# RWKV inverse in a backbone step: the transposed half made by transposes on the whole array, and three groups staggered

## The reference, cut to what matters

```python
def step(S, inp):
    r_t, w_t, k_t, v_t, kk_t, a_t = inp
    S = (S * w_t[:, :, None, :]
         - jnp.einsum('bhvk,bhk->bhv', S, kk_t)[..., None] * (kk_t * a_t)[:, :, None, :]
         + v_t[..., None] * k_t[:, :, None, :])
    return S, jnp.einsum('bhvk,bhk->bhv', S, r_t)
```

## Time and profile before

| | |
|---|---|
| time, median of 3 runs | 2682.11 us (2679.97 to 2689.62) |
| the profiled execution: its time | 2688.59 us |
| its span | 2686.8 us, 60164 instructions |
| PE busy | 2465.4 us (92%), 26965 matmuls |
| DVE / ACT / POOL busy | 1139.0 / 550.7 / 243.6 us |
| mean granted clock of PE, share of full speed | 0.977 |
| one lap of the RWKV loop (first L1367 to the next lap's) | 1382.68 to 1457.06, 74.38 us |

### The profile page before, as it was taken

The page is one execution under the profiler, slowest core; times in us unless marked ns, Lnnn a source line. Parts: engine busy times, 40 slices in busy tenths (PEclk is TensorE's granted clock), DMA queues, the critical chain, the costliest instruction groups (busy, mean ns, idle before and its releaser), DMA issues.

```text
span 2686.8 us, 60164 instructions
## 1 busy us (share of the span) xinstructions
PE 2465.4 (92%) x26965; PEld 1887.9 (70%) x26965; DVE 1139.0 (42%) x2084; ACT 550.7 (20%) x1099; POOL 243.6 (9%) x166
## 2 busy tenths in 40 slices
PE   6999889999999989987888888879899999999995
PEld 3666566777776757746667776766789778987794
DVE  4534687554563366646555555626300000000004
ACT  3101222000010020025545445431200000000002
POOL 0000240000000000003333222120100000000001
PEclk9999999999999999999999999998999999999997
DMA  8640133321221112310000000003366565656554
GB/s 353 264 185 32 48 137 133 131 79 63 72 88 60 64 57 102 127 71 4 23 23 23 23 23 24 6 20 143 125 221 214 206 220 209 239 195 221 203 202 151
DMA packets 59027, 321.20 MB, mean 120 GB/s; under 512 B 8368, under 2 KB 17968, under 8 KB 28208
## 3 DMA queue, kind: packets, MB, share of 16 engines
q1 hardware_dynamic: 46304, 281.32, 28.7%
q10 hardware_dynamic: 9040, 19.67, 1.9%
q0 software_dynamic: 3456, 16.78, 1.6%
HBM read 288.38 MB, written 29.36 MB: 118 GB/s over the span
## 4 chain that ended last, share of the span: by engine, by line
PE 85%; DVE 6%; issue 4%; ACT 3%; DMA 2%; SPq 0%; POOL 0%; DVEq 0%; ACTq 0%; POOLq 0%
PE PS L1008 36%; PE PS L1672 17%; PE PS L1696 6%; PE PS L1697 3%; PE PS L1270 2%; PE PS L1410 2%; PE PS L1416 1%; PE PS L1340 1%; PE PS L1390 1%; PE PS L971 1%; PE PS L1480 1%; PE PS L674 1%; DMA arena<-in_k 1%; PE PS L1401 1%; PE PS L1105 1%
## 5 line engine op out<-in xcount | busy, mean ns | idle before, releaser
L1008 PE MATMUL PS<-arena,ring 128*128 128x320 f32 x2680 | 742.4, 435 | 18.7 <-DVE arena L2635 13.4
L1008 PEld LDWEIGHTS PS<-arena,ring 128*128 128x128 f32 x2680 | 509.2, 191 | 239.5 <-issue 17.8
L1672 PE MATMUL PS<-arena,ring 128*128 128x192 f32 x2816 | 461.1, 327 | 4.0 <-issue 4.0
L1672 PEld LDWEIGHTS PS<-arena,ring 128*128 128x128 f32 x2816 | 458.8, 190 | 7.0 <-issue 7.0
L2911 DVE TENSOR_TENSOR arena<-arena,PS 128x192 f32<-128x192 f32 x88 | 31.1, 354 | 435.7 <-ACT arena L2119 435.7
L1696 PE MATMUL PS<-ring,arena 128*128 128x512 f32 (+1 forms) x384 | 155.1, 559 | 0.5 <-DMA ring<-in_exd 0.5
L1008 PE MATMUL PS<-arena 128*128 128x320 f32 x536 | 151.1, 432 | 0.0
L1008 PEld LDWEIGHTS PS<-arena 128*128 128x128 f32 x536 | 101.9, 190 | 42.4
L1696 PEld LDWEIGHTS PS<-ring,arena 128*128 128x128 f32 x384 | 71.6, 190 | 74.8 <-issue 71.9
L909 POOL TENSOR_TENSOR arena<-arena,const 128x512 f32<-128x512 f32 (+1 forms) x24 | 23.1, 962 | 1090.4 <-DVE arena L2738 752.1
L2119 ACT ACTIVATE arena<-PS 128x192 f32<-128x192 f32 x88 | 29.0, 330 | 420.9 <-PE PS L1672 420.9
(11 more groups left out here) (356 smaller groups left out, 3208.5 us busy)
## 6 DMA issues: line engine op xcount, KB each, us to landing
ring<-in_k SPq DMA_DIRECT2D x145, 1024.0 KB, 4.8
arena<-in_k SPq DMA_DIRECT2D x47, 1024.0 KB, 11.4
ring<-in_exd SPq DMA_DIRECT2D x32, 1408.0 KB, 5.9
ring<-in_ffd SPq DMA_DIRECT2D x8, 1408.0 KB, 5.9
rkv_s<-arena ACTq DMA_DIRECT2D x24, 320.0 KB, 4.3
expert_rows<-arena POOLq DMA_DIRECT2D x4, 1536.0 KB, 10.3
x<-in_x SPq DMA_DIRECT2D x2, 2560.0 KB, 9.7
expert_rows<-arena ACTq DMA_DIRECT2D x8, 512.0 KB, 2.6
```

The source lines that it names most:

```text
L1008: m = pe.matmul(out, lhs[:, k], rhs[:, k], start=k == 0, stop=k == count - 1)
L1672: m = pe.matmul(PS[:, k % 4, t * CAP:(t + 1) * CAP], w[:, kt, t * P:(t + 1) * P], xe[:, kt], start=kt == 0, stop=kt == KT - 1)
```

## The change

The transposed half of the inverse is no longer carried along by products of its own. X is kept for a pair of units side by side (a 128x128 block: two units by two heads), and in each level ten transposes of whole 128x128 blocks (four, four and two for the groups) turn it (`turn_inverse`, L1370 of the changed file). ACT copies the turned block out, and the products that make the next X (L1381; L1383 at level 64) use it. The products L1416 and the start by `xt`, M and `sides` go, and with them the two halves in every second level. The steps of a level are no longer in blocks by kind; the table `TURNS` gives their order over the groups, on PE and on ACT. Heads and units are placed on the array's quarters by another rule (`heads[r]`, bank `+ h`) in Y, X, `Q` and `MV`.

```diff
+TURNS = (("Y", 0), ("Y", 1), ("T", 0), ("Y", 2), ("T", 1), ("X", 0), ("T", 2), ("X", 1), ("X", 2))
...
-        XX = r(UNITS, 2, HD)
+        XX = r(UNITS // 2, 2, 2, HD)
...
+        inverse = lambda v: XX[:, v // 2, 0, v % 2]
+        turned_inverse = lambda v, h: XX[heads[v % 2], v // 2, 1, (v ^ h) % 2]
+        beside = lambda v, h: v - v % 2 + h
...
-                    masks.wait(pool, f"off2{i}", j)
-                    masks.done(pool.tensor_tensor(of_pair(XX[:, :, 1], i), eyes(i), of_pair(LTm[:, 0], i), ALU.subtract), f"xt{i}")
...
-                                m = pe.matmul(PS[hs, b + r, k * HD:(k + 1) * HD], QR[hs, unit_at(u, h), 0], eye_of(hs), start=True, stop=True)
+                                m = pe.matmul(PS[heads[r], b + h, k * HD:(k + 1) * HD], QR[hs, unit_at(u, h), 0], eye_of(hs), start=True, stop=True)
...
-                for h, hs in enumerate(heads):
-                    moved = pe.matmul(PS[hs, 6 + i % 2, 0:n * HD].rearrange("p (k m) -> p k m", k=n), eye_of(token(1, h)), of_pair(XX[:, :, 1], i)[token(1, h), 1], start=True, stop=True)
-                inv_pe.done(moved, f"M{i}")
...
             def correction(j, lv, i):
...
-                            m = pe.matmul(PS[inverse_at(i, k, h, lap), b, k * HD:(k + 1) * HD], LTm[token(u, h), OFF[lv] % 3, u], XX[token(u, h), u, 0], start=True, stop=True)
+                            m = pe.matmul(PS[heads[r], 2 * i + h, k * HD:(k + 1) * HD], LTm[token(v, h), OFF[lv] % 3, v], inverse(v)[token(v, h)], start=True, stop=True)
...
+            def turn_inverse(j, lv, i):
+                inv_dve.wait(pe, f"Y{lv}{i}", j)
+                for k, v in enumerate(PAIRS[i][0]):
+                    m = pe.transpose(PS[:, 2 * i, k * P:(k + 1) * P], XX[:, v // 2, 0].rearrange("p r n -> p (r n)"), cst("ident"))
+                inv_pe.done(m, f"T{lv}{i}")
...
             def double(j, lv, i):
+                inv_act.wait(pe, f"T{lv}{i}", j)
...
-                            m = pe.matmul(PS[token(u, h), b, k * HD:(k + 1) * HD], XX[at, u, 1], BY[at, u], start=True, stop=True)
-                inv_pe.done(m, f"X{lv}{i}")
-                for k, r in by_turns(i):
...
-                        m = pe.matmul(PS[inverse_at(i, k, h, lap + 1), 2 * i + turns_side(i, k), 256 + slot * HD:256 + (slot + 1) * HD], BY[at, u], XX[at, u, 1], start=True, stop=True)
-                inv_pe.done(m, f"Z{lv}{i}")
+                            by = BY[heads[r], beside(v, h)]
+                            if lv < 64:
+                                m = pe.matmul(PS[token(v, h), 2 * i + r, k * HD:(k + 1) * HD], turned_inverse(v, h), by, start=True, stop=True)
+                            else:
+                                m = pe.matmul(PS[heads[r], 2 * i + (r ^ h), k * HD:(k + 1) * HD], by, turned_inverse(v, h), start=True, stop=True)
+                inv_pe.done(m, f"X{lv}{i}" if lv < 64 else f"Z{lv}{i}")
...
-                    for i in range(3):
-                        correction(j, lv, i)
-                    if nxt and lv < 16:
-                        lora_mm(j + 1, {4: "w_hi", 8: "a_hi"}[lv])
-                    for i in range(3):
-                        double(j, lv, i)
+                    for ph, i in TURNS:
+                        {"Y": correction, "T": turn_inverse, "X": double}[ph](j, lv, i)
+                        if nxt and lv < 16 and (ph, i) == ("Y", 2):
+                            lora_mm(j + 1, {4: "w_hi", 8: "a_hi"}[lv])
...
             def doubled(j, lv):
...
+                for ph, i in TURNS:
+                    if ph == "Y":
+                        continue
+                    ph = phase(ph, lv)
+                    inv_pe.wait(act, f"{ph}{lv}{i}", j)
...
+                    inv_act.done(act.activation(dst, src, ACT.Copy), f"{ph}{lv}{i}")
...
-                sides(j)
```

More of the change, by code:

```diff
@@ L184 @@
         "dve": [f"{k}{i}" for k, i in PIECES if k not in BYACT]}
[L185 to L187 removed]
+MASKS = [f"off2{i}" for i in range(3)] + ["off4", "off8", "Ark", "off16", "off32", "off64"]
+TURNS = (("Y", 0), ("Y", 1), ("T", 0), ("Y", 2), ("T", 1), ("X", 0), ("T", 2), ("X", 1), ("X", 2))
+phase = lambda ph, lv: "Z" if ph == "X" and lv == 64 else ph
+INV = {"pe": [f"Y2{i}" for i in range(3)] + [f"{phase(ph, lv)}{lv}{i}" for lv in LEVELS for ph, i in TURNS],
+       "act": [f"{phase(ph, lv)}{lv}{i}" for lv in LEVELS for ph, i in TURNS if ph != "Y"],
        "dve": [f"Y{lv}{i}" for lv in (2,) + LEVELS for i in range(3)]}
@@ L390, in build @@
         y_normed = lambda j: T6 if j + 1 < KT else T1
-        WU = XX
+        WU = XX.rearrange("p m a r n -> p (m a) r n")
         PT = BY
@@ L407, in build, with pairs_of_group @@
         piece_bank = lambda n: 6 * (n % 2)
[L410 to L426, removed]
+        inverse = lambda v: XX[:, v // 2, 0, v % 2]
+        turned_inverse = lambda v, h: XX[heads[v % 2], v // 2, 1, (v ^ h) % 2]
+        beside = lambda v, h: v - v % 2 + h
+        def pairs_of_group(a, i):
             if i == 2:
-                return a.rearrange("p (d c) n -> p d c n", d=2)[:, :, 8:10]
-            return a[:, 10 * i:10 * i + 8].rearrange("p (t s) n -> p t s n", t=2)
+                return a.rearrange("p (d c) r n -> p d c r n", d=2)[:, :, 4]
+            return a[:, 5 * i:5 * i + 4]
         def of_pair(a, i):
@@ L1393, in double @@
             def double(j, lv, i):
-                inv_dve.wait(pe, f"Y{lv}{i}", j)
-                lap, n = LEVELS.index(lv), len(PAIRS[i][0])
-                if lv == 64:
+                inv_act.wait(pe, f"T{lv}{i}", j)
+                for k in range(len(PAIRS[i][0])):
                     for r in range(2):
[L1398 to L1401, removed]
-                    inv_pe.done(m, f"Z{lv}{i}")
-                    return
@@ L1422, in solve @@
                     for r in range(2):
-                        u = PAIRS[i][r][k]
-                        for h, hs in enumerate(heads):
-                            m = pe.matmul(PS[token(u, h), 2 * i + r, k * P:(k + 1) * P], XX[hs, u, 1], QM[hs, u].rearrange("p a n -> p (a n)"), start=True, stop=True)
+                        v = PAIRS[i][r][k]
+                        for h in range(2):
+                            m = pe.matmul(PS[token(v, h), 2 * i + r, k * P:(k + 1) * P], turned_inverse(v, h), QM[heads[r], beside(v, h)].rearrange("p a n -> p (a n)"), start=True, stop=True)
                 post_pe.done(m, f"WU{i}")
@@ L2750, in corrected @@
                         chain_pe.wait(dve, "y", j - 1)
-                    for ks, swapped in halves_of(i, LEVELS.index(lv) if lv > 2 else 0):
-                        eye = cst("eye64").unsqueeze(1).unsqueeze(1).to_broadcast([P, 2, ks.stop - ks.start, HD])
-                        m = dve.tensor_tensor(of_pair(XX[:, :, 0] if lv == 2 else BY, i)[:, ::-1 if swapped else 1, ks], eye, bank_pair(2 * i, i, HD)[:, :, ks], ALU.subtract)
-                    inv_dve.done(m, f"Y{lv}{i}")
+                    out = of_pair(BY, i) if lv > 2 else pairs_of_group(XX[:, :, 0], i).rearrange("p k r n -> p r k n")
+                    inv_dve.done(dve.tensor_tensor(out, eyes(i), bank_pair(2 * i, i, HD), ALU.subtract), f"Y{lv}{i}")
             log_decay(0, 0)
```

51 lines of the change are left out of this document (11 added, 40 removed).

## The result

The changed kernel takes 2731.88 us in the median (2729.37 to 2735.58), against 2682.61 for the kernel before over four runs. That is 1.0184 of the time before (95% interval 1.0165 to 1.0203): 49 us slower, where +28 was forecast. Cut at the first product of Y in level 4 and at the first of `solve`, the seven laps with work for a next lap spend 277.3 us in their levels instead of 224.8, +52.5; the stretch from the first L1351 (before: L1374, among L1367) to level 4 is 0.8 longer in the mean of these laps, +5.4, and in the last lap +1.8; the pieces give back 1.4 in all; the last lap's levels take 26.8 instead of 34.6, -7.8. Together +50.5, near the 49.3 between the medians. The profiled executions differ by less (spans 2686.8 and 2727.6), since the one of before, 6.5 above its median, spent 11 us more behind the last lap's levels, with the granted clock at 0.50 from 1803.9 to 1827.8.

The account below looks back on a forecast made before the run. It took the old levels as bound by the supply of instructions. Seven laps +26, last lap -8 and clock +10 gave +28 us: median 2682.1 becomes 2710. Range 2656 to 2738; the likeliest case's own, 2692 to 2738.

Parts of the forecast that it names:

- the clock: Granted clock falling to 0.50 around waits in levels 4 and 64: 1.5 us in seven laps, +10 us, bounds 0 and 24.
- their sums: Middle lap's levels 4 to 64, priced 8.2, 8.15, 7.7, 4.8, 7.9: 36.75 against 32.60 us, +4.15 a lap.
- "issue" went: Sign in the levels' chain: less time in which TensorE waited for no engine, 20.3% before, 31.7% in the last lap.
- X waits for L1978 in levels 4, 8, 16 and 64: Sign: TensorE's X waiting for ScalarE's copy of turned blocks takes the place of "issue".
- `Q` shows 32 records in 0.69: Q in the pieces, on four quarters: 0.69 instead of 1.15 us per 32 records, -0.4 a lap, bounds 0 to -1.2.
- The last lap's 26.8 for 26.4: Last lap's levels, no foreign work: 24.7 plus 1.7 for the clock, 26.4 against 34.60 us, -8 us.
- the staggering lets the groups cover each other: A level without foreign work: groups overlap, so it lasts 4.1 to 5.5 us; 4.8 taken.
- the longer chain of a level: Each level's group goes product, subtraction, transpose, copy, product, copy: together 4.1 us for one group.
- the supply of instructions alone decides: Rival, levels: supply decides, not the chain; -22 over seven laps, -8 in the last, -30: 2652 us, chance 0.16.
- Half the waits: Rival, levels: ScalarE's delays cost +2 a lap instead of 4.15, clock never falls: 2687 us, no change; chance 0.21.
- The new order of quarters: Rival, levels: it does not run four at a time, +1.15 a level, 46 us: 2756 us; chance 0.06.
- transposes hold the levels at 0.50: Rival, levels: transposes don't hold the clock up, up to 160 us more: about 2850 us; chance 0.03.

Follow-up runs that it names:

- e7: Changed kernel plus six unread 128x128 constant products ahead of the first X of levels 4 and 64: 2712.75 us (1.0112 of before).
- e10: e5 plus eight unread products of 128x128 constants in TensorE's waits before and among a lap's last pieces: 2644.61 us (0.9865 of before).
- e8: Changed kernel, still staggered, with the lora products w_hi and a_hi behind the second Y instead of the third: 2700.16 us (1.0071 of before).
- e4: Changed kernel with only the table TURNS altered, to blocks: all Y, all T, all X: 2674.02 us (0.9963 of before).
- e5: e4 with w_hi and a_hi behind the second Y, key_square between the rates, the gate copy behind level 64's copies: 2654.99 us (0.9903 of before).
- e3: Kernel before the change with the copy in gate moved behind the copies of level 64: 2688.43 us (1.0014 of before).
- e11: e5 with the change's staggered TURNS table instead of blocks, nothing else: 2674.36 us (0.9967 of before).
- e9: e4 plus 160 records of 16 columns a lap, ahead of X products in levels 16 and 32: 2705.13 us (1.0082 of before).
- e1: Changed kernel, only ScalarE's list altered: next lap's activations behind turned copies, gate copy behind level 64: 2689.86 us (1.0019 of before).

## Why the prediction was right, and where it was off

The time lies in the range, near its upper end of 2738, and on the side forecast, and the mechanism is the one given. Without a fall of the clock the levels came within 0.25 us of their sums: 8.36 for 8.2, 8.18 for 8.15, 7.81 for 7.7, 5.04 for 4.8, and 8.08 for 7.9 in level 64 of e7. "issue" went, two packets fewer were fetched, X waits for L1978 in levels 4, 8, 16 and 64, and `Q` shows 32 records in 0.69 (L1331, as in the row below). The last lap's 26.8 for 26.4 is partly luck: e7 has 26.25 there without any fall in its levels, where my levels add up to 24.7, and the 1.7 that I had added for the clock made up for that.

```profile
1391.27 0.69 PE L1331 MATMUL PS<-const,arena 64*64 64x64 f32 x32
```

**The term that was furthest off is the clock**, "I take 1.5 us in each of seven laps, +10 us, bounds 0 and 24". Levels 4, 8 and 64 of the seven laps are 15 us longer than in e7, which has no fall there, and the start of the lap, where I took 0 to -0.3 for the removal of M, lost 7 us (5.4 and 1.8) in the laps to falls. That is some 22 us, inside my bounds but twice what I took. Level 64 had a fall in each of the seven laps; its last products, priced at 2.8, took 4.0 with T2 between them, and 2.84 in e7. Why the clock falls at the start of seven laps, and of only three in the kernel before, no run shows; e10 shows that filler in the waits before it ends these falls.

The other 10 of the 22 us between the +28 of the sum and the +50 of the stretches are small. The five levels without a fall are 0.73 a lap over their sum of 36.75, which makes 5. The third lap, 32.60, is 0.5 longer than the mean of the seven laps before, which makes 3.4. The pieces gave 1.4, where I took 2.8 for `Q`. Two slips change nothing: the six prices of one group's chain add up to 4.04, not 4.1, and the earlier trace rows ends level 64 at 1418.66, 0.1 behind the first product of `solve`.

**The step that was too kind to the change** is "the staggering lets the groups cover each other". The same kernel in blocks has its free level at 4.32 where I gave 4.8 to the staggered one, which needed 5.04. TensorE is busy longer in pieces (4.70 for 4.21 in level 32; what the splitting costs and what the changes of form between 64x64 and 128x128 cost was not run apart), T2 stands inside X, and the third Y, and with it w_hi, a_hi and ScalarE's rates, come later. I had the late w_hi in the sum (2.5) but took it for a property of ScalarE's list; e8 shows that it is one of the staggering. That the longer chain of a level is a cost of its own falls with e4 and e5: the rest of the change, in blocks, is 9 us below before, and 28 with ScalarE's list out of the way. What e5's other two moves would do in the kernel before was not run; e3 tried the copy in `gate` alone.

The rivals: that the supply of instructions alone decides, with 2652, fails in this order of steps even where ScalarE's list is out of the way: e11 has 2674. Only in blocks does e5 come near it, with 2655. Half the waits had +2 a lap in the levels; without the falls they took +5.4. The new order of quarters runs four at a time: 32 records of X take 0.69, as in the rows of level 4. That transposes hold the levels at 0.50 is out: levels 8, 16 and 32 have ten each at 1.00. The Trainium skill, "TensorE: Matmul & The Clock Gate", section "Part 4: PE-mode transpose", says that the full clock doesn't engage for them; no run here bears that out. The about 275 ns that it gives are near the duration of one in the changed kernel, 292 in the row below, but not their distance, as ten stand in 1.31 us (e4_blocks):

```profile
L1370 PE MATMUL PS<-const,arena 128*128 128x128 f32 x50 | 8.9, 292 | 2.0 <-DVE arena L2711 2.0
```

Open is how much of the supply a level can lay up while TensorE waits; e9 shows only that it is not all.

## What to carry to other kernels

When a handoff is added in the middle of a stage, look at what stands ahead of it on the in-order engine that serves it, and at what is late behind a thing that you move back (e1's level 32). Staggering is paid in shorter pieces with changes of form between them and in everything that the moved steps push back: price it against the blocks, in a stage that has no other work. A new wait of TensorE can have a second price in the clock behind it (here 1.0 to 1.5 us, behind waits of 1.66 and 1.97 but not in every lap), and work that nobody reads can be cheaper than the wait.

## What the runs showed that I had not expected

Eight products of constants, an estimated 1.7 us of work in waits (six in about 1.3), made the start of a lap 1.1 to 1.5 us shorter where the clock had fallen, though part of that came back as time in the levels. 160 records of 16 columns a lap cost 31 us in a kernel whose levels, at 128 records in 3.7 us, had 6 us to spare in each lap (31.1 less 869 x 3.7 / 128). And a table of nine entries that sets the order of three kinds of steps is worth 58 us of 2732.
